# Seven-product weight preparation and the differences of B21 in the first group: another order on VectorE, another pair of buffers

## Chip, cores, metric

One core of one Trainium2 chip runs the kernel. The metric is device time in microseconds for one execution; several executions give a median. TensorE is PE, VectorE DVE, ScalarE ACT, GpSimd POOL, SyncE SP in every view.

## What is computed

One encoder layer over a prompt of 256 and a sample of 1024 tokens (1280 rows of 1024 values, float32): half of a SwiGLU feed-forward, a mixer, half of a second feed-forward, a last norm. The change touches only the two feed-forwards:

```python
def swiglu(h, w_gate, w_up, w_down):
    return (jax.nn.silu(h @ w_gate) * (h @ w_up)) @ w_down
x = x + 0.5 * swiglu(rmsnorm(x, norm_ffn1[l]), w_ffn1_gate[l], w_ffn1_up[l], w_ffn1_down[l])
x = x + hybrid_mixer(rmsnorm(x, norm_mix[l]), ...)
x = x + 0.5 * swiglu(rmsnorm(x, norm_ffn2[l]), w_ffn2_gate[l], w_ffn2_up[l], w_ffn2_down[l])
```

D_FF is 2816, worked off in 11 groups of 256 columns.

## The kernel before, in words

**Number format.** Every float32 operand is held as two fp32r parts, hi (ACT casts it) and lo (DVE or POOL subtracts hi from the value). A product takes three matmuls: hi x hi, hi x lo, lo x hi (L2914 to L2916; where both halves fit in 512 columns, L2912 does two of them at once).

**Products.** Gate and up projections use seven products of half-size blocks in place of eight. A *unit* q is one block column of one matrix: q even is gate, q odd is up, two units make a group. In the first group (q = 0 and 1) both use seven whole products, in the order `GU_FIRST = (GP1, GP6, GP2, GP7, GP5, GP4, GP3)`. A *step* s is one product of one unit, so steps 0 to 6 are unit 0, steps 7 to 13 unit 1. A *turn* (s, c) is one step for one part c of the columns: c = 0 has 384 and c = 1 has 256 columns in feed-forward 1, the other way round in feed-forward 2. PE's order is `GORDER`: turns (0..4, 0), then (0..4, 1), then (5,0), (5,1), (6,0), (6,1), (7,0) and so on. Turn (7, c) is GP1 of unit 1, (8, c) GP6, (9, c) GP2.

**Around a turn.** A step needs a weight block: raw weights, or a sum of them. Each unit has four weight sums (`g_sums`: L2247, L2249, L2253, L2257, all on DVE, 128x512), then ACT's `g_hi` (L1614) and DVE's `g_lo` (L2186). `g_prepare(f, n)` is g_lo, then g_sums, for block n. After a turn, DVE adds PSUM to the running result (`g_evict`, L2299), ACT copies GP1's result out of PSUM (`g_evict`, L1635, tile first_p or second_p) or takes the silu (L1654). PE's rules (`g_step`) for the turns at issue: (5, c) waits for the addition of (3, c); (6, c) for the addition of (4, c), the fifth step's; (8, c) for that of (5, c); (12, c) for that of (10, c); (9, c) for ACT's copy of (7, c), and in the part where matmuls are wide also for DVE's addition to it (L2277). All engines run their own list in order: on DVE and ACT the loops `gate_up` walk GORDER and put behind each turn its evictions, then blocks, then pieces. `FIRST_BLOCKS` says behind which of the first turns DVE prepares blocks 5 to 8; later blocks follow `G_AFTER`.

**Pieces of B21.** From group 1 on, one of the up unit's products is itself made of seven smaller ones. Their activation operands come from one block of the activations, B21 (`b21(f, e, k, half, a, b)`: part e is hi or lo, quarter (k, half)). Three of the seven are quarters themselves; four are differences, named T1 to T4 here (pieces 2, 3, 4, 5): T1 = (0,1) - (0,0), T2 = (1,1) - T1, T3 = (1,1) - (0,1), T4 = (1,0) - T2. Before the change POOL makes all of them (`piece_sum`, L1424, L1428, L1433, from hi and lo parts one after the other, 128x640 each; in feed-forward 2 every one is cut in a 256 and a 384 wide instruction). ACT casts hi (`piece_hi`, L1663), POOL rounds lo (`piece_lo`, L1441), and ACT's queue stores both to memory (`piece_store`, L1667). There are two buffers, each with a sum (piece_sum) and a hi/lo pair (piece). Who reuses a buffer waits until its old piece is stored. `PIECE_AT` and `STORES_AT` say behind which turn (q, product, c) ACT casts and stores.

Of the kernel before, what the change touches and what calls it, by code (L numbers as in the profile page):

```python
# [280 lines left out]
def build(nc, x_prompt, x_sample, norm_ffn1, w_ffn1_gate, w_ffn1_up, w_ffn1_down, norm_mix, w_in, attn_sink,  # L281
# [4 lines left out]
    with ctx:  # L286
# [1040 lines left out]
        def _(pool):  # L1327
# [77 lines left out]
            def piece_sum(f, m):  # L1405
# [19 lines left out]
                last.then_inc(pool_marks, 1)
                pool.wait_ge(*inner_pool(f, "b_sum", m, 0))
                for a, b in B21_PARTS[f]:
                    last = nc.gpsimd.tensor_tensor(to[:, :, a:b, :], to[:, :, a:b, :], b21(f, 1, *x, a, b), ALU.add)  # L1428
                last.then_inc(pool_marks, 1)
                if y:  # L1430
                    pool.wait_ge(*inner_pool(f, "b_sum", m, 1))
# [1925 lines left out]
```

## Time and profile before

| | |
|---|---|
| median of 3 runs | 2168.07 us |
| lowest, highest | 2165.01, 2168.92 us |
| the profiled execution's own time | 2166.59 us |
| its span (first to last instruction) | 2164.8 us |
| granted TensorE clock, mean | 0.999 |
| busy: PE, PEld, DVE, ACT, POOL | 2127.7, 1913.1, 1611.5, 870.7, 409.1 us |

Every time in the rows below is counted from the span's start. Feed-forward 1 begins its first unit at about 34 us, feed-forward 2 at about 1352 us. "Idle before <-releaser" is time in which the engine stood still before that instruction, and what ended it. The end of a matmul is modelled, so the idle time of PE is slightly too short.

### The profile page before, as it was taken

How to read it: one execution, taken by the hardware profiler on the slowest of the kernel's cores; microseconds unless marked ns; L12 is line 12 of the kernel's file. 1: busy time of each engine (PE TensorE's matmuls, PEld its weight loads, DVE VectorE, ACT ScalarE, POOL GpSimd, SP SyncE). 2: the span in 40 equal slices, each digit the busy share in tenths (PEclk: the TensorE clock that was granted, in tenths of full speed). 3: DMA queues.
4: the chain of work that ended last, by engine and by line, in shares of the span. 5: the costliest groups of instructions: out<-in, count | busy, mean ns of one | idle time of the engine just before them, and what ended most of it. 6: DMA issues, size and time to landing. Idle time of an engine off the chain costs nothing.

```text
span 2164.8 us, 33662 instructions
## 1 busy us (share of the span) xinstructions
PE 2127.7 (98%) x11996; PEld 1913.1 (88%) x11996; DVE 1611.5 (74%) x2904; ACT 870.7 (40%) x1716; POOL 409.1 (19%) x382
## 2 busy tenths in 40 slices
PE   6999999999999999999999999999999999999998
PEld 6899999999988888888888888899999999988887
DVE  7878888888766686988754556878887888857676
ACT  7333333333343355755543334433333333343343
POOL 7511111211100002201002344712111111100000
PEclk9999999999999999999999999999999999999999
DMA  4755565555686566433255972455554556687554
GB/s 128 219 171 173 174 210 197 195 189 197 224 304 207 175 205 170 126 109 96 93 149 171 291 231 101 132 197 191 190 200 167 178 170 212 207 300 257 173 185 166
DMA packets 283240, 402.15 MB, mean 186 GB/s; under 512 B 42498, under 2 KB 178050, under 8 KB 283076
## 3 DMA queue, kind: packets, MB, share of 16 engines
q1 hardware_dynamic: 253124, 289.90, 42.2%
q10 hardware_dynamic: 29952, 110.11, 14.3%
q8 instruction: 97, 1.59, 0.3%
q14 instruction: 67, 0.55, 0.1%
HBM read 298.04 MB, written 97.65 MB: 183 GB/s over the span
## 4 chain that ended last, share of the span: by engine, by line
PE 91%; DVE 4%; DMA 1%; issue 1%; ACT 1%; SPq 0%; POOL 0%; ACTq 0%; POOLq 0%; DVEq 0%
PE ps L2916 13%; PE ps L2912 10%; PE ps L2924 8%; PE ps L2925 8%; PE ps L2926 8%; PE ps L2914 8%; PE ps L2915 8%; PE ps L2813 4%; PE ps L2815 4%; PE ps L2814 4%; PE ps L2864 2%; PE ps L2866 2%; PE ps L2865 2%; PE ps L2831 2%; PE ps L2833 2%; PE ps L2832 2%
## 5 line engine op out<-in xcount | busy, mean ns | idle before, releaser
L2924 PE MATMUL ps<-w_hi,dh 128*128 128x512 f32 x770 | 300.2, 390 | 0.0
L2926 PE MATMUL ps<-w_hi,dh 128*128 128x512 f32 x770 | 299.7, 389 | 0.0
L2916 PE MATMUL ps<-hs,w_lo 128*128 128x384 f32 (+1 forms) x864 | 265.8, 308 | 0.0
L2361 DVE TENSOR_TENSOR dh<-dr,dh 128x640 fp32r<-128x640 f32 x154 | 128.6, 835 | 158.4 <-ACT dh L1703 158.1
L2925 PE MATMUL ps<-w_lo,dh 128*128 128x512 f32 x610 | 237.3, 389 | 0.0
L1703 ACT CAST dh<-dr 128x640 fp32r<-128x640 f32 x154 | 112.0, 727 | 261.3 <-PE ps L2926 234.1
L1614 ACT CAST w_hi<-w_raw 128x512 fp32r<-128x512 f32 x156 | 96.6, 619 | 252.2 <-PE ps L2866 170.5
L2914 PE MATMUL ps<-hs,w_hi 128*128 128x384 f32 (+1 forms) x564 | 188.0, 333 | 7.6 <-DVE first_u L2299 3.8
L2915 PE MATMUL ps<-hs,w_hi 128*128 128x384 f32 (+1 forms) x564 | 187.6, 333 | 0.0
L2912 PE MATMUL ps<-hs_first,w_hi 128*128 128x512 f32 x508 | 183.5, 394 | 0.4 <-DVE second_u L2299 0.4
L2912 PE MATMUL ps<-hs,w_hi 128*128 128x512 f32 x508 | 181.7, 391 | 0.0
L2915 PE MATMUL ps<-hq,w_hi 128*128 128x384 f32 x536 | 179.8, 335 | 0.0
L2926 PEld LDWEIGHTS ps<-w_hi,dh 128*128 128x128 f32 x770 | 144.5, 188 | 30.3
L2924 PEld LDWEIGHTS ps<-w_hi,dh 128*128 128x128 f32 x770 | 144.5, 188 | 30.0
L2916 PEld LDWEIGHTS ps<-hs,w_lo 128*128 128x128 f32 x864 | 162.7, 188 | 0.0
L2813 PE MATMUL ps<-h_hi,w_hi 128*128 128x512 f32 (+1 forms) x432 | 156.9, 363 | 0.0
L2914 PE MATMUL ps<-hq,w_hi 128*128 128x384 f32 x448 | 150.7, 336 | 3.7 <-DVE second_u L2299 2.6
L2815 PE MATMUL ps<-h_hi,w_lo 128*128 128x512 f32 (+1 forms) x432 | 153.3, 355 | 0.0
L2814 PE MATMUL ps<-h_lo,w_hi 128*128 128x512 f32 (+1 forms) x432 | 153.2, 355 | 0.0
L1614 ACT CAST w_hi<-w_sum 128x512 fp32r<-128x512 f32 x132 | 81.2, 615 | 143.9 <-DVE w_sum L2257 80.1
L2186 DVE TENSOR_TENSOR w_lo<-w_sum,w_hi 128x512 fp32r<-128x512 f32 x106 | 87.8, 828 | 65.5 <-ACT w_hi L1614 65.5
L2925 PEld LDWEIGHTS ps<-w_lo,dh 128*128 128x128 f32 x610 | 114.5, 188 | 23.3
(362 smaller groups left out, 5356.7 us busy)
## 6 DMA issues: line engine op xcount, KB each, us to landing
in_b<-inner_mid ACTq DMA_DIRECT2D x140, 640.0 KB, 5.3
dr<-hid_mid SPq DMA_DIRECT2D x154, 320.0 KB, 3.3
...
```

The lines of the kernel that those rows point to most:

```text
L1614: nc.scalar.copy(g_block(s)[0][:, 0:k, :], src).then_inc(B["hi"], 1)
L2361: v.tensor_tensor(a_lo, DR[f][n % D_HID][:, :], a_hi.bitcast(F32), ALU.subtract).then_inc(W["a_lo"], 1)
L2813: mm(out, hi, rhs_hi, start=first, stop=False)
L2814: mm(out, hi, rhs_lo, start=False, stop=False)
L2815: return mm(out, lo, rhs_hi, start=False, stop=last)
L2912: mm(ps[:, G_BANKS[j][c], :], hi[:, k, :], h_both(f, j, c, k), start=begins, stop=False, skip_group_check=True)
L2914: mm(out, hi[:, k, :], b_hi, start=begins, stop=False, skip_group_check=True)
L2915: mm(out, hi[:, k, :], b_lo, start=False, stop=False, skip_group_check=True)
L2916: last = mm(out, lo[:, k, :], b_hi, start=False, stop=k == 3, skip_group_check=True)
L2924: mm(out, hi, w_h, start=first and p in D_FRESH, stop=False, skip_group_check=True)
L2925: mm(out, hi, w_l, start=False, stop=False, skip_group_check=True)
L2926: return mm(out, lo, w_h, start=False, stop=last, skip_group_check=True)
```

## The change

It has three parts. (1) `FIRST_BLOCKS`: block 5 is prepared behind turn (1,1), block 6 behind (3,1), blocks 7, 8 and 9 behind (4,1), in both feed-forwards. Blocks 7 and 8 carry the first two weight sums of unit 1. Before, they stood ahead of the fifth step's addition of part 1. (2) T1 and T3 share buffer 0, T2 and T4 buffer 1. T4 is now formed from T2's hi and lo parts, so it has three additions instead of two. T1's cast goes behind turn (2,1), T4's behind (8,0); stores move to (4,1), (5,0), (8,1), (9,0). (3) T3's three differences go to DVE, behind its addition for turn (6,0).

```diff
-PIECE_AT = {(0, GP7, 1): T1, (0, GP5, 1): T2, (0, GP3, 1): T4, (1, GP7, 1): T3}
-STORES_AT = {(0, GP5, 1): T1, (1, GP1, 0): T2, (1, GP1, 1): T4, (1, GP5, 1): T3}
-PIECE_BUFFER = {T1: 0, T2: 1, T4: 0, T3: 1}
+PIECE_AT = {(0, GP2, 1): T1, (0, GP5, 1): T2, (0, GP3, 1): T3, (1, GP6, 0): T4}
+STORES_AT = {(0, GP5, 1): T1, (0, GP4, 0): T2, (1, GP6, 1): T3, (1, GP2, 0): T4}
+PIECE_BUFFER = {T1: 0, T2: 1, T3: 0, T4: 1}
+B21_T3_AT = (0, GP3, 0)
...
         def b21_read(f):
-            return (done(f, entry(1, GP2), 1), piece_stored(f, 0), inner_pool(f, "b_sum", T3, 2))
+            return (done(f, entry(1, GP2), 1), piece_stored(f, 0), inner_dve(f, "b_sum", T3, 2),
+                    inner_pool(f, "b_sum", T4, 2))
...
                 elif m == T2:
                     pool.wait_ge(*inner_pool(f, "b_sum", T1, 2))
-                elif m == T4:
-                    pool.wait_ge(*inner_pool(f, "b_sum", T2, 1))
-                    pool.wait_ge(*piece_stored(f, T1))
                 else:
                     pool.wait_ge(*piece_stored(f, T2))
...
+                def difference(a, b):
+                    t, x_hi, x_lo = to[:, :, a:b, :], b21(f, 0, *x, a, b), b21(f, 1, *x, a, b)
+                    if m == T1:
+                        y_hi, y_lo = b21(f, 0, 0, 0, a, b), b21(f, 1, 0, 0, a, b)
+                        return (t, x_hi, y_hi, ALU.subtract), (t, t, x_lo, ALU.add), (t, t, y_lo, ALU.subtract)
+                    if m == T2:
+                        return (t, x_hi, piece_value(f, T1)[:, :, a:b, :], ALU.subtract), (t, t, x_lo, ALU.add)
+                    return (t, x_lo, lo[:, :, a:b, :], ALU.subtract), (t, t, x_hi, ALU.add), (t, t, hi[:, :, a:b, :], ALU.subtract)
...
                 piece_sum(f, T2)
                 piece_lo(f, T1)
+                piece_lo(f, T2)
                 piece_sum(f, T4)
-                piece_lo(f, T2)
+                piece_lo(f, T3)
                 piece_lo(f, T4)
-                piece_sum(f, T3)
-                piece_lo(f, T3)
...
             def piece_hi(f, m):
-                act.wait_ge(*inner_pool(f, "b_sum", m, 2 if m in (T1, T3) else 1))
-                if m in (T3, T4):
-                    act.wait_ge(*piece_stored(f, {T4: T1, T3: T2}[m]))
+                if m == T3:
+                    act.wait_ge(*piece_stored(f, T1))
+                    act.wait_ge(*inner_dve(f, "b_sum", T3, 2))
+                else:
+                    act.wait_ge(*inner_pool(f, "b_sum", m, 1 if m == T2 else 2))
...
+            def third_difference(f):
+                dve.wait_ge(*piece_stored(f, T1))
+                to = piece_value(f, T3)
+                for n in range(3):
+                    if n:
+                        dve.wait_ge(*inner_dve(f, "b_sum", T3, n - 1))
+                    for a, b in B21_PARTS[f]:
+                        t = to[:, :, a:b, :]
+                        if n == 0:
+                            last = v.tensor_tensor(t, b21(f, 0, 1, 1, a, b), b21(f, 0, 0, 1, a, b), ALU.subtract)
+                        else:
+                            last = v.tensor_tensor(t, t, b21(f, 1, 2 - n, 1, a, b), ALU.add if n == 1 else ALU.subtract)
+                    last.then_inc(L["dve"], 1)
...
-            FIRST_BLOCKS = ({1: (5, 6), 3: (7, 8)}, {1: (5, 6), 2: (7,), 3: (8,)})
+            FIRST_BLOCKS = {(1, 1): (5,), (3, 1): (6,), (4, 1): (7, 8, 9)}
...
+                    if (q, j, c) == B21_T3_AT:
+                        third_difference(f)
```

**Order on DVE, feed-forward 1, from block 5's weight sum on.** In the changed file L2257 is L2275, L2186 is L2190, L2299 is L2317, L2247 and L2249 are L2265 and L2267. first_u3 is the running result of steps 3 and 4. Before:

```order
L2257 TENSOR_TENSOR w_sum1<-w_raw0,w_sum1 128x512
L2186 TENSOR_TENSOR w_lo0<-w_sum1,w_hi0 128x512
L2299 TENSOR_TENSOR first_u3<-ps,first_p1 128x256
L2186 TENSOR_TENSOR w_lo1<-w_raw2,w_hi1 128x512
L2247 TENSOR_TENSOR w_sum0<-w_raw0 128x512
L2249 TENSOR_TENSOR w_sum1<-w_sum0,w_raw2 128x512
L2186 TENSOR_TENSOR w_lo1<-w_sum1,w_hi1 128x512
L2299 TENSOR_TENSOR first_u3<-ps,first_u3 128x256
```

Now:

```order
L2275 TENSOR_TENSOR w_sum1<-w_raw0,w_sum1 128x512
L2317 TENSOR_TENSOR first_u3<-ps,first_p1 128x256
L2190 TENSOR_TENSOR w_lo0<-w_sum1,w_hi0 128x512
L2317 TENSOR_TENSOR first_u3<-ps,first_u3 128x256
L2190 TENSOR_TENSOR w_lo1<-w_raw2,w_hi1 128x512
L2265 TENSOR_TENSOR w_sum0<-w_raw0 128x512
L2267 TENSOR_TENSOR w_sum1<-w_sum0,w_raw2 128x512
L2190 TENSOR_TENSOR w_lo1<-w_sum1,w_hi1 128x512
```

The additions for turns (3,1) and (4,1) moved ahead of one and of four weight instructions.

**Order on DVE, feed-forward 1, at the additions for step 6** (first_u2 is their result). Now:

```order
L2190 TENSOR_TENSOR w_lo0<-w_raw2,w_hi0 128x512
L2275 TENSOR_TENSOR w_sum1<-w_raw2,w_sum1 128x512
L2317 TENSOR_TENSOR first_u2<-ps,first_u2 128x384
L2219 TENSOR_TENSOR piece_sum0_0<-hs 128x640
L2221 TENSOR_TENSOR piece_sum0_0<-piece_sum0_0,hs 128x640 x2
L2317 TENSOR_TENSOR first_u2<-ps,first_u2 128x256
```

Before, the same list stood there without the three 128x640 rows; the rest of it has not moved.

**Order on ACT, feed-forward 1, between the silu of turn (5,0) and the copies of (7,0) and (7,1)** (sg is the silu's target, first_p the copies'). Before:

```order
L1654 ACTIVATE sg<-first_p 128x384 [waits gateup_added]
L1654 ACTIVATE sg<-first_p 128x256 [waits gateup_added]
L1614 CAST w_hi<-w_raw 128x512 [waits block_summed,gateup_done]
L1654 ACTIVATE sg<-first_u 128x384 [waits gateup_added]
L1654 ACTIVATE sg<-first_u 128x256 [waits gateup_added]
L1614 CAST w_hi<-w_sum 128x512 [waits block_summed,gateup_done]
L1663 CAST piece_0<-piece_sum_0 128x640 [waits gla_o_ld0,pool_marks]
L1635 COPY first_p<-ps 128x384 [waits gateup_silu,gateup_done]
L1667 DMA inner_mid<-piece_1 128x1280 [waits pool_marks]
L1635 COPY first_p<-ps 128x256 [waits gateup_silu,gateup_done]
```

Now:

```order
L1656 ACTIVATE sg<-first_p 128x384 [waits gateup_added]
L1671 DMA inner_mid<-piece_1 128x1280 [waits pool_marks]
L1656 ACTIVATE sg<-first_p 128x256 [waits gateup_added]
L1616 CAST w_hi<-w_raw 128x512 [waits block_summed,gateup_done]
L1656 ACTIVATE sg<-first_u 128x384 [waits gateup_added]
L1656 ACTIVATE sg<-first_u 128x256 [waits gateup_added]
L1616 CAST w_hi<-w_sum 128x512 [waits block_summed,gateup_done]
L1667 CAST piece_0<-piece_sum_0 128x640 [waits inner_dve,gla_o_ld0]
L1637 COPY first_p<-ps 128x384 [waits gateup_silu,gateup_done]
L1637 COPY first_p<-ps 128x256 [waits gateup_silu,gateup_done]
```

T2's store moved up to the silus of step 5. The cast ahead of the copies waits for T3 from DVE (inner_dve) where it waited for T4 from POOL (pool_marks).

## Rows read from the trace of the kernel before

**Rows 1.** The page of the profiled execution: span and busy time.
```profile
span 2164.8 us, 33662 instructions
...
PE 2127.7 (98%) x11996; PEld 1913.1 (88%) x11996; DVE 1611.5 (74%) x2904; ACT 870.7 (40%) x1716; POOL 409.1 (19%) x382
```

**Rows 2.** Timeline of PE, feed-forward 1: start us, us, instruction, [idle before <-releaser].
```profile
59.01 0.35 PE L2914 MATMUL ps<-hs,w_hi 128*128 128x256 f32 x1 [0.68 <-DVE first_u L2299]
...
65.10 0.36 PE L2914 MATMUL ps<-hs,w_hi 128*128 128x256 f32 x1 [2.33 <-DVE first_u L2299]
...
70.08 0.34 PE L2914 MATMUL ps<-hs,w_hi 128*128 128x384 f32 x1
...
74.83 0.41 PE L2914 MATMUL ps<-hs,w_hi 128*128 128x384 f32 x1 [1.12 <-ACT first_p L1635]
...
86.33 0.41 PE L2914 MATMUL ps<-hs,w_hi 128*128 128x384 f32 x1 [0.82 <-DVE first_u L2299]
```

**Rows 3.** Timeline of PE, feed-forward 2.
```profile
1383.87 0.41 PE L2914 MATMUL ps<-hq,w_hi 128*128 128x384 f32 x1 [2.62 <-DVE second_u L2299]
...
1384.55 0.53 PE L2914 MATMUL ps<-hq,w_hi 128*128 128x384 f32 x1
...
1398.04 0.39 PE L2912 MATMUL ps<-hs_first,w_hi 128*128 128x512 f32 x1
```

**Rows 4.** Engines in one stretch; PEclk is the granted TensorE clock.
```profile
core 0: us, PE busy (x) PEld busy (x) DVE busy (x) ACT busy (x) POOL busy (x), PEclk, DMA share, GB/s
...
1384.50:1387.60 3.10, 3.10 (x11) 3.10 (x11) 2.00 (x3) 1.85 (x4) 3.10 (x3) 0.50 0.71 159
```

**Rows 5.** Timeline of DVE, feed-forward 1.
```profile
60.57 1.89 DVE L2247 TENSOR_TENSOR w_sum<-w_raw 128x512 f32<-128x512 f32 x1
62.49 0.69 DVE L2249 TENSOR_TENSOR w_sum<-w_sum,w_raw 128x512 f32<-128x512 f32 x1
...
64.53 0.42 DVE L2299 TENSOR_TENSOR first_u<-ps,first_u 128x256 f32<-128x256 f32 x1
...
67.22 0.88 DVE L2299 TENSOR_TENSOR first_p<-ps,first_p 128x384 f32<-128x384 f32 x2
...
70.39 0.88 DVE L2299 TENSOR_TENSOR first_u<-ps,first_u 128x384 f32<-128x384 f32 x2
...
96.67 0.81 DVE L2332 TENSOR_TENSOR st<-sg 128x640 f32<-128x640 f32 x1
```

**Rows 6.** Timeline of POOL, feed-forward 1.
```profile
60.01 1.90 POOL L1428 TENSOR_TENSOR piece_sum<-piece_sum,hs 128x640 f32<-128x640 f32 x1
64.59 1.56 POOL L1441 TENSOR_TENSOR piece<-piece_sum,piece 128x640 fp32r<-128x640 f32 x1 [2.68 <-ACT piece L1663]
70.26 1.64 POOL L1424 TENSOR_TENSOR piece_sum<-hs,piece_sum 128x640 f32<-128x640 f32 x1 [4.11 <-DMA inner_mid<-piece]
...
78.57 1.58 POOL L1424 TENSOR_TENSOR piece_sum<-hs 128x640 f32<-128x640 f32 x1 [1.53 <-DMA inner_mid<-piece]
```

**Rows 7.** Timeline of ACT, feed-forward 1.
```profile
66.18 0.34 ACTq L1667 DMA_DIRECT2D inner_mid<-piece  x1
...
73.58 0.72 ACT L1663 CAST piece<-piece_sum 128x640 fp32r<-128x640 f32 x1 [1.27 <-POOL piece_sum L1428]
74.22 0.47 ACT L1635 COPY first_p<-ps 128x384 f32<-128x384 f32 x1
```

**Rows 8.** Instructions of tile piece, whole span: store to landing.
```profile
DMA to landing us min/median/max: 2.9/3.0/3.9
```

**Rows 9.** Timeline of POOL, feed-forward 2.
```profile
1384.20 1.08 POOL L1428 TENSOR_TENSOR piece_sum<-piece_sum,hs_first 128x256 f32<-128x256 f32 x1
1385.23 1.01 POOL L1428 TENSOR_TENSOR piece_sum<-piece_sum,hq 128x384 f32<-128x384 f32 x1
```

**Rows 10.** Timelines of ACT and of DVE, feed-forward 2.
```profile
1387.78 0.33 ACTq L1667 DMA_DIRECT2D inner_mid<-piece  x1
...
1392.56 0.87 DVE L2299 TENSOR_TENSOR second_u<-ps,second_u 128x256 f32<-128x256 f32 x2
```

More of the change, by code:

```diff
@@ L195, in inner_marks @@
     act, dve = [], []
-    pool = [("b_sum", T1, 0), ("b_sum", T1, 1), ("b_sum", T1, 2), ("b_sum", T2, 0), ("b_sum", T2, 1), ("b_lo", T1),
-            ("b_sum", T4, 0), ("b_sum", T4, 1), ("b_lo", T2), ("b_lo", T4),
-            ("b_sum", T3, 0), ("b_sum", T3, 1), ("b_sum", T3, 2), ("b_lo", T3)]
+    pool = [("b_sum", T1, 0), ("b_sum", T1, 1), ("b_sum", T1, 2), ("b_sum", T2, 0), ("b_sum", T2, 1), ("b_lo", T1), ("b_lo", T2),
+            ("b_sum", T4, 0), ("b_sum", T4, 1), ("b_sum", T4, 2), ("b_lo", T3), ("b_lo", T4)]
     for s, c in GORDER:
@@ L223, in inner_marks @@
             act += [("b_hi", PIECE_AT[(q, j, c)])]
+        if (q, j, c) == B21_T3_AT:
+            dve += [("b_sum", T3, n) for n in range(3)]
     return act, dve, pool
@@ L1425, in piece_sum @@
[L1425 to L1431, printed above, removed]
-                    for a, b in B21_PARTS[f]:
-                        last = nc.gpsimd.tensor_tensor(to[:, :, a:b, :], to[:, :, a:b, :], b21(f, 1, *y, a, b), ALU.subtract)
+                to, hi, lo = piece_value(f, m), *(by_pair(PIECE[f][PIECE_BUFFER[m]][:, e, :, :].bitcast(F32)) for e in range(2))
@@ L1434, in piece_sum @@
+                parts = [difference(a, b) for a, b in B21_PARTS[f]]
+                for n in range(len(parts[0])):
+                    if n:
+                        pool.wait_ge(*inner_pool(f, "b_sum", m, n - 1))
+                    for part in parts:
+                        last = nc.gpsimd.tensor_tensor(*part[n])
                     last.then_inc(pool_marks, 1)
@@ L1437, in piece_lo @@
                 pool.wait_ge(*inner_act(f, "b_hi", m))
-                if m == T2:
-                    pool.wait_ge(*inner_pool(f, "b_sum", T4, 1))
+                if m == T1:
+                    pool.wait_ge(*inner_pool(f, "b_sum", T2, 0))
                 to = PIECE[f][PIECE_BUFFER[m]]
@@ L2326, in hid_sums @@
                         dve.wait_ge(*piece_stored(f, T3))
+                        dve.wait_ge(*piece_stored(f, T4))
                     dve.wait_ge(*gated(f, entry(2 * i + 1, GP4 if i else GP3), 1))
@@ L2411, in gate_up @@
                     g_mult(f, s, c)
-                    if s < G_LEAD - 1:
-                        for n in FIRST_BLOCKS[f].get(s, ()):
+                    if s < G_LEAD:
+                        for n in FIRST_BLOCKS.get((s, c), ()):
                             g_prepare(f, n)
@@ L2422, in gate_up @@
                         d_prepare(f, s + D_LEAD + 1 - G_STEPS)
+                    if (q, j, c) == B21_T3_AT:
+                        third_difference(f)
                     if q and q % 2 == 0 and j in (GP1, GP6):
```

8 lines of the change are left out of this document (2 added, 6 removed).

## Prediction

> **What bounds the kernel now.** I read the page first, then the waits and the timeline of PE, then the timelines of DVE, POOL and ACT in the two stretches that the change touches. PE is busy 2127.7 us of a span of 2164.8 [rows 1], so only about 37 us of idle time can be won, and a PE wait that grows is paid in full. In feed-forward 1 the stretch has four gaps [rows 2]. Turn (5,1) waits 0.68 us and turn (6,1) waits 2.33 us, both for additions on DVE. Turn (9,0) waits 1.12 us for ACT's copy of turn (7,0). Turn (12,0) waits 0.82 us for an addition. In feed-forward 2 there is one gap, 2.62 us ahead of turn (5,1) at 1383.87, and its matmuls from 1384.55 on take 0.53 instead of 0.34 us [rows 3]: for 3.1 us the granted clock is 0.50, the 1.2 GHz level, with PE at work for all of it [rows 4]. That gap therefore cost 2.6 us and another 3.1 x 0.5 = 1.55 us, more than any other here.
>
> The rows to look at next are DVE's durations. A 128x512 sum with both operands in SBUF takes 0.69 us at 62.49, but 1.89 us at 60.57 [rows 5]. POOL's instruction that began at 60.01 ended at 61.91 [rows 6], and DVE's ended at 62.46, 0.55 us later. So a DVE instruction with two SBUF operands does its work only when POOL's running instruction is over. POOL pays too: 1.90 us where it takes 1.56 alone [rows 6]. The additions from PSUM are untouched (0.42 at 64.53 [rows 5]). Where both engines have such work, they alternate, one instruction each.
>
> **Part 1, the order on DVE.** Nothing is added; two additions go ahead of weight work. The first weight sum of unit 1 still starts at 60.57 [rows 5], where the raw weights are in, and the additions for (3,1) and (4,1) now stand ahead of it, done by about 59. Turns (5,1) and (6,1) need not wait: -3.0 us by the time of (7,0). In feed-forward 2 it is -2.6 and, as the gap is gone, -1.55 for the clock. What is late next is turn (8,0): it needs the addition for (5,0), which still stands behind all the weight work. It ended near 67.7 before [rows 5]. DVE saves its wait for the late silu, but the sum at 62.49 now meets POOL's rounding of T1, which ACT's earlier cast releases, and takes 1.3 us longer. I put that addition at 67.9 as before, so (8,0) starts at 68.1 instead of 70.08 [rows 2]: 2.0 of the 3.0 us are left there.
>
> **Part 2, the buffers.** T2's store moves between ACT's two silus of step 5. It waits for POOL's rounding of T2, that one for the cast of T2 behind the casts of blocks 8 and 9. In feed-forward 1: T1's store at about 66.9 (66.18 before [rows 7]), T2's rounding 1.56 us plus a turn of DVE, so its store issues at 69.1. ACT stands still for it, then needs a silu and the cast of block 10 (0.4 + 0.55), DVE the rounding, the weight sum and the addition for (6,0) (0.6 + 0.6 + 0.5): done at 72.0. Before, that pair of additions began at 70.39 [rows 5]. POOL has two instructions fewer in the whole part. That is worth nothing by itself, since POOL is nobody's bound, but T3's three, from 78.57 on [rows 6], no longer hold DVE up, so I take the 0.82 us ahead of (12,0) as gone.
>
> **Part 3, T3 on DVE.** Three additions of 128x640 with both operands in SBUF come between the additions for (6,0) and (6,1). The nearest row for one is 0.81 us [rows 5], so 2.5 us if POOL is quiet. If each has to let one of POOL's go first, it is POOL's 1.5 and its own work, 0.55 x 640/512 = 0.68 us: 2.2 each, 6.5 in all. POOL's differences for T4 start when T2 is stored: issue at 69.1 plus 2.9 to 3.9 us [rows 8], so at 72.0 to 73.2 (T1's took 4.1 us from issue to POOL's next start [rows 6, 7]), just when DVE starts at 72.0. I take the first as free and two as alternating: 0.8 + 2 x 2.2 = 5.2, with 2.5 and 6.5 as ends. T3 is ready at 77.2. Behind it, in order: the addition for (6,1), its silu, the cast of block 11, the cast of T3, the copy of (7,0), at 0.4 + 0.45 + 0.5 + 0.65 + 0.5 us (cast and copy overlap as at 73.58 and 74.22 [rows 7]), and 0.2 to PE. **Turn (9,0) starts at 79.9 instead of 74.83** [rows 2]: +5.1 us. What was won at (5,1) and (6,1) lies inside this and is gone.
>
> Sum for feed-forward 1: +5.1 - 0.8. PE now stands still from 71.6 to 79.9, and the only clock drop in these rows followed a shorter gap. I add one such stretch, +1.55 (bounds 0 and 3.1). Result +5.85.
>
> Feed-forward 2 goes the same way. T1's store stood at 1387.78 [rows 10], T2's rounding is another 1.56 behind it, and POOL has lost up to 1.5 us to DVE by then: T2's store at 1391.0, the thirds from 1394.0 (the additions of step 6 stood at 1392.56 [rows 10]). They are six instructions, 256 and 384 wide. Alone they take about 0.85 a pair. POOL's 384 wide one takes 1.01 us [rows 9], a 256 wide one two thirds of it (the 1.08 beside it has DVE's share in it), and DVE's own work is 0.68 split in 0.3 and 0.4. With POOL's differences due from 1394.1 on, an alternating pair costs 0.7 + 0.3 + 0.95 + 0.4 = 2.35. First pair free: 0.85 + 2 x 2.35 = 5.5 (ends 2.6 and 7.0). Then 3.0 us of the same tail, which here also has DVE's addition to the copy. Turn (9,0) starts at 1402.5 instead of 1398.04 [rows 3]: +4.5, in which the old clock loss is already credited; a new one costs +1.55. Result +6.0.
>
> Together +11.9 us: 2166.59 becomes 2178.5 for the profiled execution. The median lies 1.5 above it; by the median it is 2180.0. **I forecast 2179 us**, between the two.
>
> A rule of the Trainium skill bears on the thirds (SBUF — State Buffer, section Who interferes with whom). By it a DVE instruction with two SBUF inputs and a GpSimd instruction that reads SBUF exclude each other, and "Issue order, not op shape, decides who blocks." Read as "the engine that came first keeps going", the rule would let DVE's three differences pass ahead of POOL's, and the sum would be +6.3 instead of +11.9, which is the first rival below. The alternation at 60 to 62 us speaks for my reading.
>
> **The rivals.**
> - *Slower, but without contention.* POOL's T4 comes after DVE is through, or DVE holds its place. Then T3 costs 2.5 and 2.6 us: (9,0) at 77.2 and at 1399.6. That is +2.4 - 0.8 + 1.55 and +1.6 + 1.55, together +6.3; without new clock drops +3.2. So 2171 to 2174 us. For it: the store's landing varies by 1 us and could end late. Against it: both start within 0.2 us by my sum, and only three free ones give it. Chance 0.2.
> - *Faster.* The cast of T3 does not hold up ACT's copy. That is decided by one number: T3 would have to be ready by 72.1 us in feed-forward 1 (74.83 less the 2.7 us behind it), as early as I have it begin. Each us earlier than that is won, up to all of 0.68 + 2.33 + 1.12 + 0.82 + 2.62 + 1.55 = 9.1 us, or 2159. For it: at this very place ACT waited until 73.58 for POOL's two differences of T4 [rows 7], which began at 70.26 [rows 6]; three on DVE at 0.8 from the same start would be done at 72.8, and DVE's weight work may end earlier than I think. Against it: T1's store lands at 70 us or later, and the addition for (6,0) is no earlier than before. Chance 0.08.
> - *The change does not do what it says.* The fifth step's addition could still come late. The order shows it four instructions earlier, so only the size of part 1 is open, not its sign. No chance of its own.
> - *No visible change.* Gains and losses cancel, with T3 ready near 73 to 74 us. It shares its ground with the uncontended case without clock drops. Chance 0.12.
>
> **How the numbers follow.** Forecast case 0.6, uncontended 0.2, cancelling 0.12, faster 0.08. About 0.2% (4.3 us) is what a measurement of this kernel can tell from no change. The forecast case and three quarters of the uncontended case lie above it: slower 0.75, within 0.17, faster 0.08. The range: at the top all differences alternate (+1.3, +1.5) and a clock drop lasts twice as long (+1.55), which gives about 2184; at the bottom it takes in most of the uncontended case, 2169.5.
>
> **What would show it right or wrong.** On PE's timeline the gaps ahead of (5,1) and (6,1) in feed-forward 1 and ahead of (5,1) in feed-forward 2 vanish. A short gap ahead of (8,0) appears, and a long one, 6 to 9 us, ahead of (9,0) in both, released by ACT's copy; matmuls behind it run for some 3 us at a granted clock of 0.50. The 128x640 differences on DVE show about 0.8 us once and about 2.2 us twice. On ACT the cast of piece stands idle for DVE's piece_sum. It would be wrong if (9,0) started by 75 us, or if all three differences took 0.8 us, or if PE came through a gap of 6 us or more at full clock.

## Result and the profile after

The changed kernel takes 2175.92 us, median of 5 runs (2175.39 to 2180.05), the kernel before 2167.65 us in 5 runs (2165.01 to 2168.92). The ratio is 1.0044, 95% interval 1.0032 to 1.0056: slower by 8.3 us. The profiled execution took 2175.51 us and its span is 8.7 us longer than that of before [rows 1]. The page of the changed kernel:

```profile
span 2173.5 us, 33665 instructions
...
PE 2128.9 (98%) x11996; PEld 1914.9 (88%) x11996; DVE 1617.9 (74%) x2913; ACT 871.0 (40%) x1716; POOL 402.2 (19%) x376
```

Otherwise the page reads like that of before. PE is busy 1.2 us longer; the other 7.5 of the 8.7 us are idle time. The timeline of PE, changed kernel, feed-forward 1 and then 2 (start us, us, instruction, [idle before <-releaser]):

```profile
67.51 0.41 PE L2935 MATMUL ps<-hs,w_hi 128*128 128x384 f32 x1 [1.19 <-DVE first_p L2317]
...
77.54 0.66 PE L2935 MATMUL ps<-hs,w_hi 128*128 128x384 f32 x1 [6.32 <-ACT first_p L1637]
...
1394.48 0.47 PE L2933 MATMUL ps<-hs_first,w_hi 128*128 128x512 f32 x1 [0.42 <-DVE second_p L2317]
...
1405.61 0.77 PE L2933 MATMUL ps<-hs_first,w_hi 128*128 128x512 f32 x1 [7.42 <-DVE second_p L2295]
```

These are all the gaps in the two stretches. Those ahead of (5,1), (6,1) and (12,0) [rows 2] and ahead of (5,1) in feed-forward 2 [rows 3] are gone. New are 1.19 and 0.42 us ahead of (8,0), and ahead of **(9,0) stand 6.32 and 7.42 us** in place of 1.12 and none. Engines in the stretches around these two, with the granted clock as the third figure from the right:

```profile
core 0: us, PE busy (x) PEld busy (x) DVE busy (x) ACT busy (x) POOL busy (x), PEclk, DMA share, GB/s
71.00:77.50 6.50, 0.22 (x2) 0.00 (x0) 5.06 (x6) 2.55 (x6) 4.68 (x3) 0.74 0.46 139
77.50:80.60 3.10, 3.06 (x10) 3.09 (x11) 2.77 (x6) 1.93 (x4) 3.10 (x3) 0.50 0.06 17
80.60:84.00 3.40, 3.40 (x20) 3.24 (x19) 1.57 (x4) 0.89 (x2) 1.86 (x1) 0.95 1.03 365
1405.60:1408.70 3.10, 3.09 (x10) 2.71 (x11) 2.73 (x5) 1.60 (x4) 2.49 (x2) 0.50 0.53 185
```

Behind both waits PE works for 3.1 us at a granted clock of 0.50, the 1.2 GHz level, as in [rows 4]. In feed-forward 2 it is back after these 3.1 us, in feed-forward 1 after another 0.3 (0.95 over the stretch from 80.60). Half of the time at 0.50 is lost: 1.55 and 1.7 us. DVE, feed-forward 1, from the rounding that follows T2's store (T3's differences are L2219 once and L2221 twice; each of the three is asked for by itself):

```profile
69.68 0.69 DVE L2190 TENSOR_TENSOR w_lo<-w_raw,w_hi 128x512 fp32r<-128x512 f32 x1 [1.98 <-ACT w_hi L1616]
70.29 0.68 DVE L2275 TENSOR_TENSOR w_sum<-w_raw,w_sum 128x512 f32<-128x512 f32 x1
70.89 0.55 DVE L2317 TENSOR_TENSOR first_u<-ps,first_u 128x384 f32<-128x384 f32 x1
71.36 0.81 DVE L2219 TENSOR_TENSOR piece_sum<-hs 128x640 f32<-128x640 f32 x1
72.21 0.82 DVE L2221 TENSOR_TENSOR piece_sum<-piece_sum,hs 128x640 f32<-128x640 f32 x1
73.06 2.04 DVE L2221 TENSOR_TENSOR piece_sum<-piece_sum,hs 128x640 f32<-128x640 f32 x1
75.03 0.41 DVE L2317 TENSOR_TENSOR first_u<-ps,first_u 128x256 f32<-128x256 f32 x1
```

POOL, same stretch, T4's first two differences:

```profile
72.67 1.75 POOL L1436 TENSOR_TENSOR piece_sum<-hs,piece 128x640 f32<-128x640 f32 x1 [4.35 <-DMA inner_mid<-piece]
74.50 1.99 POOL L1436 TENSOR_TENSOR piece_sum<-piece_sum,hs 128x640 f32<-128x640 f32 x1
```

ACT, same stretch:

```profile
68.34 0.33 ACTq L1671 DMA_DIRECT2D inner_mid<-piece  x1
68.72 0.42 ACT L1656 ACTIVATE sg<-first_p 128x256 f32<-128x256 f32 x1 [0.79 <-POOL piece L1444]
...
75.47 0.42 ACT L1656 ACTIVATE sg<-first_u 128x256 f32<-128x256 f32 x1 [3.47 <-DVE first_u L2317]
75.79 0.60 ACT L1616 CAST w_hi<-w_sum 128x512 fp32r<-128x512 f32 x1
76.30 0.72 ACT L1667 CAST piece<-piece_sum 128x640 fp32r<-128x640 f32 x1
76.93 0.74 ACT L1637 COPY first_p<-ps 128x384 f32<-128x384 f32 x2
```

The chain can be read off. ACT stands still 0.79 us at T2's store (68.34) for POOL's rounding; so the cast behind it is late, and DVE waits 1.98 us for that cast at 69.68. The addition of (6,0), 70.89, lets T3's differences go from 71.36 to 75.10. Only then come the addition for (6,1), ACT's silu of it (3.47 us idle), two casts, and the copy at 76.93 that releases turn (9,0). The differences begin while POOL is idle: the first two take 0.81 and 0.82 us. The third starts at 73.06, when POOL's instruction of 72.67 is under way, and ends at 75.10; that is POOL's end, 72.67 + 1.75 = 74.42, plus 0.68 us. DVE in feed-forward 2, the last pair and the addition behind it:

```profile
1399.11 1.34 DVE L2221 TENSOR_TENSOR piece_sum<-piece_sum,hq 128x384 f32<-128x384 f32 x1
1400.49 0.83 DVE L2221 TENSOR_TENSOR piece_sum<-piece_sum,hs_first 128x256 f32<-128x256 f32 x1
1401.24 1.34 DVE L2221 TENSOR_TENSOR piece_sum<-piece_sum,hq 128x384 f32<-128x384 f32 x1
1402.51 0.54 DVE L2317 TENSOR_TENSOR second_u<-ps,second_u 128x384 f32<-128x384 f32 x1
```

Here four of the six differences alternate with POOL's (0.83 and 1.34 us in place of 0.42 and 0.55), 5.1 us in all.

**A ruler.** Executions differ before the change begins: the first addition of step 3 is at 49.50 us here and at 49.92 before. So I measure every profile from marks. The first mark is DVE's addition for turn (3,0), the second is a turn of PE at the head of feed-forward 2, before the change acts there; these are the marks in the trace of before (DVE, then PE):

```profile
49.92 0.55 DVE L2299 TENSOR_TENSOR first_u<-ps,first_p 128x384 f32<-128x384 f32 x1
```

```profile
1358.65 0.39 PE L2914 MATMUL ps<-hs_first,w_hi 128*128 128x256 f32 x1 [0.40 <-DVE w_lo L2186]
```

In the table each row is one kernel of the experiments below. "Start" is the first mark, FF1 the way from it to the second, FF2 from there to the end of the span, (9,0) that turn from the mark ahead of it; all in us against the kernel before (49.92; 1308.73; 806.15; 24.91 and 39.39). The three bold columns add up to the difference in span.

| kernel | **start** | (9,0) in FF1 | **FF1** | (9,0) in FF2 | **FF2** | median us (runs) | ratio to before, 95% interval |
|---|---|---|---|---|---|---|---|
| changed | -0.42 | +3.1 | +4.2 | +3.8 | +4.9 | 2175.92 (5) | 1.0044 [1.0032, 1.0056] |
| order only | +0.3 | +0.1 | +0.4 | -1.2 | +0.8 | 2167.80 (11) | 1.0003 [0.9994, 1.0012] |
| pieces only | -0.1 | +5.6 | +5.5 | +3.8 | +6.3 | 2178.33 (5) | 1.0049 [1.0036, 1.0062] |
| T3 on POOL | -0.3 | +0.9 | +2.8 | +0.6 | +2.6 | 2171.84 (7) | 1.0023 [1.0012, 1.0034] |
| same, cast behind | +1.2 | +0.3 | +2.1 | +0.1 | +2.0 | 2170.99 (11) | 1.0019 [1.0010, 1.0028] |
| no overlap | +0.1 | +1.9 | +3.4 | +1.4 | +3.2 | 2175.91 (5) | 1.0039 [1.0026, 1.0052] |
| one difference more | +0.4 | +5.1 | +5.8 | +5.9 | +8.2 | 2181.35 (4) | 1.0065 [1.0051, 1.0079] |
| T3's cast behind | 0.0 | +2.5 | +4.6 | +3.5 | +5.5 | 2176.62 (4) | 1.0044 [1.0030, 1.0057] |
| T3 later | +1.4 | -1.1 | +0.9 | -1.3 | +0.5 | 2168.28 (11) | 1.0006 [0.9997, 1.0015] |
| T3 later, T2's store back | 0.0 | -2.0 | +3.9 | -1.5 | +2.9 | 2173.51 (5) | 1.0034 [1.0022, 1.0047] |
| same, casts behind | +1.6 | -2.0 | +4.1 | -1.6 | +3.3 | 2171.30 (10) | 1.0022 [1.0013, 1.0032] |
| order and cast | +1.3 | -2.0 | +1.2 | -1.8 | +0.8 | 2168.98 (11) | 1.0010 [1.0001, 1.0019] |
| same, store behind | | | | | | 2168.42 (10) | 1.0003 [0.9994, 1.0012] |

The four starts of +1.2 us and more go with one thing: PE's first turn of feed-forward 1 ran in part at half clock (0.65 to 0.70 over 34 to 38 us; 1.00 in the other profiles). The edits act only behind that. Of the last kernel's twelve executions two, the profiled one among them, ran at a mean granted clock of 0.654 and 0.563; they are left out, and no trace of it is read.

### The profile page after: what moved, and what is told of

It is laid out like the page before. It is cut to its first block, busy times and chain, and to the rows that moved or that the text cites. A ratio compares the mean times of both kernels' runs of the same rounds, so it can differ in the third digit from the quotient of the medians.

```text
span 2173.5 us, 33665 instructions
## 1 busy us (share of the span) xinstructions
PE 2128.9 (98%) x11996; PEld 1914.9 (88%) x11996; DVE 1617.9 (74%) x2913; ACT 871.0 (40%) x1716; POOL 402.2 (19%) x376
## 4 chain that ended last, share of the span: by engine, by line
PE 91%; DVE 4%; ACT 1%; issue 1%; DMA 1%; SPq 0%; POOL 0%; ACTq 0%; POOLq 0%; DVEq 0%
PE ps L2937 13%; PE ps L2933 10%; PE ps L2935 8%; PE ps L2936 8%; PE ps L2945 8%; PE ps L2946 8%; PE ps L2947 8%; PE ps L2834 4%; PE ps L2836 3%; PE ps L2835 3%; PE ps L2885 2%; PE ps L2887 2%; PE ps L2886 2%; PE ps L2852 2%; PE ps L2854 2%; PE ps L2853 2%
## 5 line engine op out<-in xcount | busy, mean ns | idle before, releaser
L2190 DVE TENSOR_TENSOR w_lo<-w_sum,w_hi 128x512 fp32r<-128x512 f32 x106 | 84.9, 801 | 65.1 <-ACT w_hi L1616 64.8
```

## Experiments: which part costs what

**Order only.** Part 1 put into the kernel before.

```diff
-            FIRST_BLOCKS = ({1: (5, 6), 3: (7, 8)}, {1: (5, 6), 2: (7,), 3: (8,)})
+            FIRST_BLOCKS = {(1, 1): (5,), (3, 1): (6,), (4, 1): (7, 8, 9)}
...
-                    if s < G_LEAD - 1:
-                        for n in FIRST_BLOCKS[f].get(s, ()):
+                    if s < G_LEAD:
+                        for n in FIRST_BLOCKS.get((s, c), ()):
```

> Part 1 alone: the kernel before with the new FIRST_BLOCKS, pieces as they were. Theory A (T3 on VectorE in front of the copy of turn (7,0) is the whole loss; part 1 is harmless): the gaps ahead of (5,1) and (6,1) vanish, a gap of about 1 us opens ahead of (8,0), (9,0) stays near 74.8 us in feed-forward 1, since ACT still waits until 73.5 for POOL's T4, and moves from 1398.0 to about 1396.9 in feed-forward 2. In all 1 to 2 us faster than before, about 2166. Rival B (the new order of the weight sums costs by itself, through the later block 8 and 9 and turn (8,0)): slower than before by 2 us or more, and part of the measured 8 us.

Measured: no change. Rival B falls, and theory A's gain of 1 to 2 us did not come. The gaps ahead of (5,1) and (6,1) go, but (9,0) is where it was in feed-forward 1. PE, then ACT:

```profile
75.20 0.41 PE L2914 MATMUL ps<-hs,w_hi 128*128 128x384 f32 x1 [3.26 <-ACT first_p L1635]
```

```profile
73.95 0.72 ACT L1663 CAST piece<-piece_sum 128x640 fp32r<-128x640 f32 x1 [1.33 <-POOL piece_sum L1428]
```

The whole gain waits at (9,0): there ACT's copy of (7,0) stands behind T4's cast, and that waits for POOL. In feed-forward 2, (9,0) is 1.2 us earlier, but a gap of 3.09 us stands ahead of it, and behind it PE works at a granted clock of 0.50 for 3.3 us (0.61 over 1397.5 to 1400.6, 0.85 to 1404.0): the clock loss that the gap at (5,1) had [rows 3, 4] is back. Part 1 alone is worth nothing that these times can show.

**Pieces only.** Parts 2 and 3 with the old FIRST_BLOCKS.

> Parts 2 and 3 alone: the changed kernel with the old FIRST_BLOCKS. Theory A: the chain to the copy of (7,0) is as late as in the changed kernel, so (9,0) starts at about 77.5 us again; the gaps in front of it at (5,1), (6,1) are back but lie inside its wait. 7 to 9 us slower than before, 2175 to 2177; less only if the shorter waits spare a clock drop. Rival B: about half the loss is gone, 2171 or less.

Measured: some 11 us more than before, where 7 to 9 was expected; rival B falls. With the old order (9,0) comes at 80.29 us, 2.4 us later still in feed-forward 1 by the marks, and there are gaps of 0.65, 3.56 and 3.88 us ahead of (5,1), (6,1) and (9,0). In feed-forward 2 (9,0) is where the changed kernel has it; that way is 1.3 us longer, and 0.9 of it is a stretch of 4.9 us at half clock behind (9,0) in place of 3.1. So parts 2 and 3 cost about 11 us together. That part 1 gives back 2 to 3 of them is seen in the profiles (2.7 us); the medians are 2.4 us apart, but the intervals of the two ratios overlap almost wholly, so the times don't settle it.

**T3 on POOL.** The changed kernel, but POOL makes T3's differences, behind its rounding of T2 and ahead of T4's, which thus come later. Orders on the other engines, buffers, casts and stores stay.

```diff
                 piece_lo(f, T2)
+                piece_sum(f, T3)
                 piece_sum(f, T4)
...
-                    if (q, j, c) == B21_T3_AT:
-                        third_difference(f)
```

> The changed kernel with T3's three differences made by GpSimd behind its rounding of T2 and ahead of T4's; VectorE has nothing of T3. Orders, buffers, casts and stores stay. It tells what the move to VectorE alone costs. In the changed kernel GpSimd's rounding of T2 ended at 68.3 us, so its three differences should run from there at 1.6 to 2 us each (VectorE takes turns with it) and end near 74 us in feed-forward 1. Theory A (the third difference on VectorE holds up its additions and, through ACT's cast of T3, ACT's copy of turn (7,0)): the addition for (6,1) is no longer held, but the cast of T3 still stands ahead of the copies and waits until 74 us, so turn (9,0) starts near 75.3 instead of 77.5, some 2 us less there and as much in feed-forward 2. Time about 2172. Rival E (it does not matter which engine makes T3, only when its buffer is free): (9,0) at 77.5, time within 1 us of the changed kernel's 2176.

Measured: 2171.84 us, (9,0) at 75.44 us, 2.2 and 3.2 us earlier than in the changed kernel: as theory A has it (2172, 75.3); rival E falls. PE, POOL, DVE and ACT of this kernel, feed-forward 1:

```profile
75.44 0.57 PE L2917 MATMUL ps<-hs,w_hi 128*128 128x384 f32 x1 [4.08 <-ACT first_p L1635]
```

```profile
68.37 1.56 POOL L1433 TENSOR_TENSOR piece_sum<-hs 128x640 f32<-128x640 f32 x1
70.01 3.84 POOL L1433 TENSOR_TENSOR piece_sum<-piece_sum,hs 128x640 f32<-128x640 f32 x2
```

```profile
69.78 0.71 DVE L2188 TENSOR_TENSOR w_lo<-w_raw,w_hi 128x512 fp32r<-128x512 f32 x1 [1.97 <-ACT w_hi L1614]
70.41 2.05 DVE L2259 TENSOR_TENSOR w_sum<-w_raw,w_sum 128x512 f32<-128x512 f32 x1
72.38 0.88 DVE L2301 TENSOR_TENSOR first_u<-ps,first_u 128x384 f32<-128x384 f32 x2
```

```profile
74.20 0.72 ACT L1665 CAST piece<-piece_sum 128x640 fp32r<-128x640 f32 x1
74.82 0.74 ACT L1635 COPY first_p<-ps 128x384 f32<-128x384 f32 x2
```

So **making T3 on DVE instead of on POOL (part 3) costs about 4 of the 8 us**: this kernel stands 4.1 us below the changed one (3.7 by the ways in the profiles) and 4.0 us above "order only". How much of these other 4 is part 2 is not settled. Two things are seen. T2's store is one: DVE's 1.97 us of idle time behind it are still there, and in the changed kernel the addition for (6,0) starts 21.39 us behind the mark (70.89 less 49.50), against 20.47 before (70.39 [rows 5] less 49.92), 0.9 us later. The other is new in this kernel: the weight sum at 70.41 takes 2.05 us instead of 0.68, because POOL now works on T3 at that place. And 1.2 us are a stretch of 5.6 us at half clock in feed-forward 2, in place of 3.3. Part 2 with T3 made by POOL behind T4, as before the change, was never run.

**Same, cast behind.** Besides, T3's cast behind turn (7,1), its rounding ahead of T4's differences, T4's cast behind (10,1), the stores behind (9,0) and (11,1).

```diff
-PIECE_AT = {(0, GP2, 1): T1, (0, GP5, 1): T2, (0, GP3, 1): T3, (1, GP6, 0): T4}
-STORES_AT = {(0, GP5, 1): T1, (0, GP4, 0): T2, (1, GP6, 1): T3, (1, GP2, 0): T4}
+PIECE_AT = {(0, GP2, 1): T1, (0, GP5, 1): T2, (1, GP1, 1): T3, (1, GP7, 1): T4}
+STORES_AT = {(0, GP5, 1): T1, (0, GP4, 0): T2, (1, GP2, 0): T3, (1, GP5, 1): T4}
```

> The kernel with T3's differences on GpSimd, and besides T3's cast by ACT behind turn (7,1), where ACT's two copies are already out of the way, its rounding ahead of T4's differences, its store behind turn (9,0); T4's cast behind (10,1), its store behind (11,1). Theory A: with nothing of the pieces between step 6's additions and the copies, turn (9,0) starts near 72.5 to 73 us in feed-forward 1 and near 1396 in feed-forward 2; the clock stays up or falls once. Time 2162 to 2165, that is 3 to 6 us less than before. Rival F (whatever is moved, VectorE and ACT only hand the wait on to the turn behind): (9,0) is early, but the time lies within 2 us of 2167.6, with new gaps at (9,1) or (12,0).

Measured: 2170.99 us, where 2162 to 2165 was expected. The cast was worth 0.6 us at (9,0) in both feed-forwards. The rest stays: T2's store between the silus and the contended weight sum hold the addition of step 6, and the gaps of 3.56 and 3.72 us still take the clock with them. Neither theory A's number nor rival F's new gap came.

## Experiments: what holds turn (9,0)

**No overlap.** POOL's differences for T4 wait for the end of DVE's for T3.

```diff
                     pool.wait_ge(*piece_stored(f, T2))
+                    pool.wait_ge(*inner_dve(f, "b_sum", T3, 2))
```

> The changed kernel with one wait added: POOL starts T4's differences only when VectorE has T3 complete. If the alternation with POOL is part of the price (theory A), the three differences take 2.4 us in all in feed-forward 1 (3.7 in the changed kernel) and 2.7 in feed-forward 2 (5.1): (9,0) 1.3 and 2.4 us earlier, 3.5 to 4 us less than the changed kernel, about 2172. Rival C (the differences are slow for another reason, or their time is hidden and only the order on ACT counts): no change, or slower through the later T4.

DVE and POOL of this kernel, feed-forward 1:

```profile
71.83 0.81 DVE L2220 TENSOR_TENSOR piece_sum<-hs 128x640 f32<-128x640 f32 x1
72.68 1.69 DVE L2222 TENSOR_TENSOR piece_sum<-piece_sum,hs 128x640 f32<-128x640 f32 x2
74.29 0.42 DVE L2318 TENSOR_TENSOR first_u<-ps,first_u 128x256 f32<-128x256 f32 x1
```

```profile
74.51 1.54 POOL L1437 TENSOR_TENSOR piece_sum<-hs,piece 128x640 f32<-128x640 f32 x1 [5.72 <-DVE piece_sum L2222]
```

Without POOL the three take 0.85 us each, 2.5 in all, and (9,0) comes 1.2 and 2.4 us earlier, as theory A has it. That is the price of the contention at (9,0). The profile's ways are only 0.8 and 1.7 us shorter. In feed-forward 1 the clock takes back half of the gain: PE works 4.7 us at 0.50 behind (9,0), in place of 3.4.

```profile
76.81:81.50 4.69, 4.69 (x15) 4.59 (x16) 2.93 (x6) 1.89 (x4) 4.61 (x4) 0.50 0.35 101
```

The median, expected at about 2172 us, is that of the changed kernel within 0.1 us, and the profiled execution was the fastest of its five. So the saving is seen in the profile and not settled by the times.

**One difference more.** One further 128x640 difference on DVE ahead of T3's, written over the hi half of T1, which is stored by then.

```diff
                 dve.wait_ge(*piece_stored(f, T1))
+                for e in range(1):
+                    spare = by_pair(PIECE[f][0][:, e, :, :].bitcast(F32))
+                    for a, b in B21_PARTS[f]:
+                        v.tensor_tensor(spare[:, :, a:b, :], b21(f, 0, 1, 1, a, b), b21(f, 0, 0, 1, a, b), ALU.subtract)
                 to = piece_value(f, T3)
```

> The changed kernel with one more 128x640 difference ahead of T3's three, written to a place that is overwritten later. Theory A: turn (9,0) moves by all of it: 0.75 us for the instruction, and 1.4 more in feed-forward 1, because one more of the three meets POOL; 0.8 to 1.7 in feed-forward 2. In all 3 to 4 us slower than the changed kernel, about 2179. Rival C: less than 0.5 us.

```profile
72.15 0.82 DVE L2215 TENSOR_TENSOR piece<-hs 128x640 f32<-128x640 f32 x1
72.89 0.82 DVE L2223 TENSOR_TENSOR piece_sum<-hs 128x640 f32<-128x640 f32 x1
73.74 4.11 DVE L2225 TENSOR_TENSOR piece_sum<-piece_sum,hs 128x640 f32<-128x640 f32 x2
```

These are DVE's rows. The added one costs 0.8 us itself and pushes the next into POOL's time: now two alternate at 2.05 us each. (9,0) is 1.9 and 2.1 us later than in the changed kernel, the time 5.4 us more where 3 to 4 were expected; rival C falls. Whatever stands between the additions for (6,0) and (6,1) is paid in full at (9,0), and more than its own 0.8 us. Of what the time has beyond (9,0), 0.5 us are a stretch at half clock of 4.1 us in feed-forward 2; the rest is not traced.

**T3's cast behind.** The changed kernel with T3's cast behind turn (7,1) instead of (6,1).

```diff
-PIECE_AT = {(0, GP2, 1): T1, (0, GP5, 1): T2, (0, GP3, 1): T3, (1, GP6, 0): T4}
+PIECE_AT = {(0, GP2, 1): T1, (0, GP5, 1): T2, (1, GP1, 1): T3, (1, GP6, 0): T4}
```

> The changed kernel with only T3's cast moved on ACT behind the copies; its differences stay between the two additions of step 6 on VectorE. Theory A (the differences hold up the second addition, so the silu and the copy behind it): only the cast's own 0.65 us is gained in each feed-forward, 1 to 2 us in all, about 2174.5. Rival D (the cast's wait on ACT is the whole matter): nearly all of the 8 us comes back.

Measured: (9,0) 0.6 and 0.3 us earlier, the time unchanged, where 1 to 2 us less was expected; rival D falls. In feed-forward 1 PE works 4.0 us at half clock behind (9,0) in place of 3.4, which takes back 0.3 us. It is the differences on DVE that hold (9,0), by way of the addition for (6,1), not the cast.

**T3 later.** T3's differences behind turn (8,1) on DVE, its cast behind (10,1), T4's behind (8,1), stores behind (11,1) and (9,1); POOL rounds T4 first.

```diff
-PIECE_AT = {(0, GP2, 1): T1, (0, GP5, 1): T2, (0, GP3, 1): T3, (1, GP6, 0): T4}
-STORES_AT = {(0, GP5, 1): T1, (0, GP4, 0): T2, (1, GP6, 1): T3, (1, GP2, 0): T4}
+PIECE_AT = {(0, GP2, 1): T1, (0, GP5, 1): T2, (1, GP7, 1): T3, (1, GP6, 1): T4}
+STORES_AT = {(0, GP5, 1): T1, (0, GP4, 0): T2, (1, GP5, 1): T3, (1, GP2, 1): T4}
...
-B21_T3_AT = (0, GP3, 0)
+B21_T3_AT = (1, GP6, 1)
...
                 piece_sum(f, T4)
+                piece_lo(f, T4)
                 piece_lo(f, T3)
-                piece_lo(f, T4)
```

> The changed kernel with T3's differences moved on VectorE from turn (6,0) to behind turn (8,1), and the casts and stores of T3 and T4 moved on ACT behind the copies of (7,0) and (7,1), T4 ahead of T3. Nothing is left out. Theory A: the chain to the copy loses the three differences and the cast: (9,0) at about 73.2 us instead of 77.5 in feed-forward 1 and 5.7 us earlier in feed-forward 2, both gaps at about 2 us, and no clock drop behind them (another 1.5 each, surely in feed-forward 1). In all 10 to 13 us less than the changed kernel and 2 to 5 less than before: 2162 to 2165. Against it would speak a new gap ahead of (10,0) or (12,0) as large as the one removed.

Measured: 2168.28 us: nearly the whole loss is gone, but nothing is won over before, where 2162 to 2165 was expected. (9,0) comes 1.1 and 1.3 us earlier than before; gaps of 2.07 and 2.33 us ahead of it are each followed by a clock drop, which eats that. T3's differences take 2.17 us and 2.93 for the other two at the new place; the gap ahead of (12,0) in feed-forward 1 is 0.84 us, as before. That the loss goes when the differences leave this place shows that it hung on them there.

## Experiments: is there a version that beats both

**T3 later, T2's store back.** "T3 later" with T2's store behind (6,0) instead of between the silus.

```diff
-STORES_AT = {(0, GP5, 1): T1, (0, GP4, 0): T2, (1, GP5, 1): T3, (1, GP2, 1): T4}
+STORES_AT = {(0, GP5, 1): T1, (0, GP3, 0): T2, (1, GP5, 1): T3, (1, GP2, 1): T4}
```

> As the kernel with T3 later, and T2's store behind turn (6,0) instead of (5,0), so that ACT does not stand between its two silus of step 5. If that stall was part of the lateness (part 2 of the prediction), the additions for step 6 come 0.8 to 1.1 us earlier in feed-forward 1 and 0 to 0.4 in feed-forward 2: about 1 us less than the kernel with T3 later. If it was not, no difference.

(9,0) comes 0.9 and 0.3 us earlier, as it should, but T4 is late with the store. POOL, ACT and PE, feed-forward 1:

```profile
76.82 1.56 POOL L1436 TENSOR_TENSOR piece_sum<-hs,piece 128x640 f32<-128x640 f32 x1 [8.06 <-DMA inner_mid<-piece]
```

```profile
82.64 0.73 ACT L1667 CAST piece<-piece_sum 128x640 fp32r<-128x640 f32 x1 [8.59 <-POOL piece_sum L1436]
83.27 0.36 ACT L1641 COPY first_u<-ps 128x256 f32<-128x256 f32 x1
```

```profile
87.80 0.66 PE L2935 MATMUL ps<-hs,w_hi 128*128 128x384 f32 x1 [4.28 <-DVE first_u L2317]
```

ACT stands 8.59 us at T4's cast, its copy behind it is late, and (12,0) waits 4.28 us, again with the clock at 0.50 behind it. 2173.51 us, 5 more than "T3 later", where 1 less was expected.

**Same, casts behind.**

```diff
-PIECE_AT = {(0, GP2, 1): T1, (0, GP5, 1): T2, (1, GP7, 1): T3, (1, GP6, 1): T4}
-STORES_AT = {(0, GP5, 1): T1, (0, GP3, 0): T2, (1, GP5, 1): T3, (1, GP2, 1): T4}
+PIECE_AT = {(0, GP2, 1): T1, (0, GP5, 1): T2, (1, GP5, 1): T3, (1, GP7, 1): T4}
+STORES_AT = {(0, GP5, 1): T1, (0, GP3, 0): T2, (1, GP4, 1): T3, (1, GP5, 1): T4}
```

> The kernel with T3 later and T2's store behind turn (6,0), and besides T4's cast behind turn (10,1) and its store behind (11,1), T3's cast behind (11,1) and its store behind (12,1). In that run turn (9,0) came at 72.88 us, but ACT stood still 8.59 us ahead of T4's cast, its copy for turn (9,1) came at 83.27 us behind it, and turn (12,0) waited 4.28 us with the clock at 0.50 behind it. Theory A: the cast is all that held the copy; the copy comes at about 77 us, the gap at (12,0) shrinks below 1.5 us, the clock stays up behind it, and feed-forward 1 gets 4 to 5 us shorter, feed-forward 2 some 2 us: time 2166 to 2168, at most 1.5 us below before. Rival F (the wait is handed on): T3's differences on VectorE, which share the time with T4's on GpSimd (76 to 82 us), hold up what (12,0) needs; the gap there stays above 3 us and the time at 2172 to 2174.

PE and DVE:

```profile
86.94 0.41 PE L2935 MATMUL ps<-hs,w_hi 128*128 128x384 f32 x1 [1.81 <-DVE first_u L2317]
...
110.88 0.66 PE L2935 MATMUL ps<-hs,w_hi 128*128 128x384 f32 x1 [2.87 <-DVE first_u L2317]
```

```profile
108.11 0.69 DVE L2265 TENSOR_TENSOR w_sum<-w_raw 128x512 f32<-128x512 f32 x1 [4.08 <-DMA w_raw<-in_w_ffn_up]
```

The gap at (12,0) shrinks to 1.81 us, but T3's differences still share their time with T4's (78.50 to 82.69 for two), and a new gap of 2.87 us with a clock drop appears in the next group, behind a landing of up weights that DVE awaits for 4.08 us. Why those weights came late I have not traced. This profile is of the slowest of the ten executions (2175.71 us; the others go down to 2169.48), so whether the new gap stands in the others is not shown. The median is 2171.30 us, between theory A's 2166 to 2168 and rival F's 2172 to 2174: the copy is free, yet little is won, and in this execution the wait is handed on.

**Order and cast.** "Order only" with T4's cast behind (7,1) and its store behind (8,0).

```diff
-PIECE_AT = {(0, GP7, 1): T1, (0, GP5, 1): T2, (0, GP3, 1): T4, (1, GP7, 1): T3}
-STORES_AT = {(0, GP5, 1): T1, (1, GP1, 0): T2, (1, GP1, 1): T4, (1, GP5, 1): T3}
+PIECE_AT = {(0, GP7, 1): T1, (0, GP5, 1): T2, (1, GP1, 1): T4, (1, GP7, 1): T3}
+STORES_AT = {(0, GP5, 1): T1, (1, GP1, 0): T2, (1, GP6, 0): T4, (1, GP5, 1): T3}
```

> The kernel before with part 1 and with T4's cast moved on ACT behind the copies of (7,0) and (7,1); all pieces on POOL as before. Theory A: what kept part 1 from showing was that cast in front of the copy. (9,0) starts at 73.0 to 73.5 us instead of 74.9 and about 0.5 us earlier in feed-forward 2, where the clock drop may stay; the 0.8 us gap ahead of (12,0) stays. 2 to 3.5 us less than before, about 2164.5. If part 1 is worth nothing by itself, no difference from before.

(9,0) is 2.0 and 1.8 us earlier than before, the earliest of all, yet the time is 2168.98 us, where about 2164.5 was expected. PE, turn (9,1), and ACT:

```profile
78.24 0.47 PE L2912 MATMUL ps<-hs,w_hi 128*128 128x512 f32 x1 [1.76 <-DVE first_p L2277]
```

```profile
77.26 0.37 ACT L1635 COPY first_p<-ps 128x256 f32<-128x256 f32 x1 [3.25 <-POOL piece L1441]
```

The other part's copy now stands behind T4's store, 3.25 us.

**Same, store behind.** T4's store behind (9,0).

```diff
-STORES_AT = {(0, GP5, 1): T1, (1, GP1, 0): T2, (1, GP6, 0): T4, (1, GP5, 1): T3}
+STORES_AT = {(0, GP5, 1): T1, (1, GP1, 0): T2, (1, GP2, 0): T4, (1, GP5, 1): T3}
```

> The kernel before with the new order of weight preparation and T4's cast behind turn (7,1), as in the run with the order and the cast, but T4's store behind turn (9,0) in place of (8,0). In that run ACT stood still 3.25 and 2.91 us for GpSimd's rounding of T4 ahead of the store, and its copy of turn (7,1) behind it ended 1.76 and 2.50 us of idle time on TensorE at turn (9,1). Theory: these two gaps go, and what follows at (12,0) changes by less than 0.5 us: time 2164 to 2166. Rival F (the wait is handed on): another gap of 1 to 2 us each takes their place and the time stays at 2168 to 2169.

Measured: 2168.42 us, 0.6 less than "order and cast", not the 3 to 5 expected. Without a profile, where the wait went stays open. No version beats the kernel before; "order only", "T3 later" and this one equal it within what the times can tell.

## Why the prediction was right, and where it was off

- **Sign, size and range.** 2179 forecast, 2175.92 measured, inside 2169.5 to 2184.5 and above the 0.2% bound. The chain was the one predicted: additions of step 6, differences, silu, cast, copy, turn (9,0), in both feed-forwards.
- **Gaps removed, (8,0).** As forecast. (8,0) was put at 68.1 us and came at 67.51, which is 67.9 with the early start added.
- **T2's store and the begin of the thirds.** Forecast 69.1 and 72.0 us, measured 68.34 and 71.36, with the start's 0.42 added 68.8 and 71.8. In feed-forward 2 the thirds were put at 1394.0; they began at 1397.44, which is 1393.7 less the 3.76 us by which this feed-forward began later (1362.41 against 1358.65).
- **The step that was mis-sized: "the first as free and two as alternating", 5.2 us.** In feed-forward 1 it was two free and one alternating, 3.7 us. POOL's first difference came 4.33 us after the store's issue and thus 1.3 us after DVE's first, not at the same time. The prediction had reckoned with the landings of [rows 8], 2.9 to 3.9 us; its own 4.1 us from T1's store to POOL's next start would have given 73.2 and two free differences. The price of an alternating one was right (2.04 us against 2.2). In feed-forward 2 the forecast was 5.5 and the measurement 5.1. So (9,0) was +3.1 instead of +5.1 (the differences 1.5 us shorter, their begin 0.2 earlier, the tail behind them 2.4 us instead of 2.7), and +3.8 instead of +4.5 (0.4 and 0.3 us).
- **Clock.** One stretch at half clock behind each wait was forecast; it is what came (0.50 for 3.4 and 3.1 us of work).
- **(12,0).** Its 0.82 us are gone, as forecast.
- **The sum.** FF1 forecast +5.85, measured +4.2; FF2 forecast +6.0, measured +4.9. The table's 9.1 us less the early start give the 8.7 of the span.
- **What the prediction did not see** is how the loss splits. It named part 3 as the cost and part 2 as a shift in time. "T3 on POOL" shows that without the move to DVE the kernel still stands 4 us above "order only": T2's store, which ACT waits at, makes the addition for (6,0) 0.9 us late, and a clock drop comes behind (9,0) in both feed-forwards. The rest of these 4 us may be that kernel's own. And it booked 3.0 us in feed-forward 1 and 4.15 in feed-forward 2 as the worth of part 1, lost again only through T3; "order only" shows that it is worth nothing even without T3's move, since T4's cast and a new clock loss hold (9,0).
- **Rivals.** The uncontended case was priced at +6.3 us; "no overlap" is that case, and its two ways are +3.4 and +3.2 in the profile, though its median stayed at 2175.91. The faster one needed T3 ready by 72.1 us; it was ready at 75.1.
- **Who goes first.** The Trainium skill (SBUF — State Buffer, section Who interferes with whom) says that issue order decides who blocks. The rows agree, taken one instruction at a time: POOL's of 72.67 us was there before DVE's third difference of 73.06 and went first, although two of DVE's had gone before. So the reading that an engine that came first keeps its turn for what follows, which the first rival rested on, does not hold here.
